# Order of dense matmuls in three FFNs of a two-layer decoder trunk

## The chip, the cores and the metric

The kernel runs on one core of one Trainium2 chip. Its time is what the device takes for one execution, in microseconds. The engines are named as the profile names them: PE is TensorE's matmul, PEld its weight load (the load of the stationary operand), DVE is VectorE, ACT is ScalarE, POOL is GpSimd and SP is SyncE, which here only starts transfers.

## The reference

The program is a trunk of two decoder layers on 256 tokens with 1024 features. A layer is an FFN, a token mixer and a second FFN, each between two RMS norms and added to the residual stream. All four FFNs compute the same, each with weights of its own:

```
def swiglu(h, wg, wu, wd):                      # wg, wu: 1024 x 2816, wd: 2816 x 1024
    return (jax.nn.silu(h @ wg) * (h @ wu)) @ wd

x = x + 0.5 * rms_norm(swiglu(rms_norm(x, pre), wg, wu, wd), post)
```

The two mixers (sliding window and latent attention in layer 0; compressed, selected, sliding and block-sparse attention in layer 1) are not touched.

## The kernel before

Everything is float32, and each dense product is computed from split operands: an operand `a` is held as `a_hi`, its copy in the chip's shorter float32 form, and `a_lo = a - a_hi`. A product of two such operands is three matmuls that add up in one PSUM bank, hi x hi, hi x lo and lo x hi. `three` (line 893) issues them for one chunk of 128 rows of the contraction. In `mm(dst, lhs, rhs, ...)` the second argument is the stationary operand (activations, 128 x 128), the third the moving one (weights, 128 x 512).

The tokens are two row tiles of 128, `t` = 0 and 1. An FFN walks through 11 blocks of 256 hidden features, `jc` = 0 to 10. In a block:

- `gate_up` (TensorE): for each row tile 8 chunks x 3 = 24 matmuls into PSUM bank 4 + t. The 512 columns are 256 of the gate and 256 of the up projection. The last matmul of a tile raises `gu_ready`.
- ScalarE applies silu to the gate half of each tile (line 679), and VectorE multiplies by the up half (line 1356), which raises `h_ready`.
- `down` of the block before (TensorE): 24 matmuls into banks 0 to 3, in two column parts of 512; within a part tile 0 and then tile 1, each 2 chunks x 3 matmuls. After each part `down_used` is raised.
- `turn_h` (TensorE): waits until both tiles of `h` are there and transposes them, 4 matmuls with the identity, into bank 6 (line 982).

TensorE's order is `gate_up(jc)`, `down(jc - 1)`, `turn_h(jc)`, and again. The last block differs: `down(9)` is cut in two by `turn_h(10)`, so that 12 down matmuls stand before the transposes. Blocks 3 to 8 are a loop with two blocks in its body; the others are written out.

Weights are loaded by SyncE, in one queue, two buffers ahead for gate/up and one for down. Each has to be split on the chip: ScalarE writes the hi part (lines 630 and 692), VectorE the lo part (lines 1281 and 1367). This work stands in a fixed order with the rest. For ScalarE it is, in block `jc` (`step` in its `ffn`): the copy of the turned `h` of block jc - 1, the two halves of its down rows, silu of tile 0, **the two halves of the gate/up weights of block jc + 1**, silu of tile 1. VectorE has the same order, with the multiply in place of silu:

```
def step(jc, g, ahead):
    if jc >= 1:
        behind(jc - 1, g)
    mul(jc, 0, g)
    if ahead:
        split_main(n0 + jc + 1, hi=g(2 * (n0 + jc + 1) + 1, 2))
    mul(jc, 1, g)
```

`ahead` is false only in block 10 of the fourth FFN, after which the program has no more gate/up weights. FFNs are numbered `u` = 0 to 3.

Of the kernel before, what the change touches and what calls it, by code (L numbers as in the profile page):

```python
# [37 lines left out]
P = 128  # L38
SEQ = 256
TILES = SEQ // P  # L40
D = 1024
KD = D // P
# [16 lines left out]
FC = FB // P  # L59
# [27 lines left out]
def trunk(nc, a, out):  # L87
# [5 lines left out]
    first_block, n = {}, 0  # L93
# [20 lines left out]
    job_base, n = {}, 0  # L114
# [12 lines left out]
    rstd_base, n = {}, 0  # L127
# [6 lines left out]
    ss_of, n = {}, 0  # L134
# [20 lines left out]
    with ExitStack() as ctx:  # L155
# [6 lines left out]
        ps = ctx.enter_context(nc.psum_tensor("ps", [P, 8, 512], F32))  # L162
# [3 lines left out]
        w_hi = sb("w_hi", [P, 2, MAIN], F32R)  # L166
        w_lo = sb("w_lo", [P, 2, MAIN], F32R)
        raw_down = sb("raw_down", [P, DOWN])
        down_hi = sb("down_hi", [P, DOWN], F32R)
        down_lo = sb("down_lo", [P, DOWN], F32R)  # L170
# [3 lines left out]
        xt_hi = sb("xt_hi", [P, KD, SEQ], F32R)  # L174
        xt_lo = sb("xt_lo", [P, KD, SEQ], F32R)
# [89 lines left out]
        main_hi, main_lo = sem("main_hi"), sem("main_lo")  # L265
        d_hi, d_lo, down_used = sem("d_hi"), sem("d_lo"), sem("down_used")
# [7 lines left out]
        gu_ready, silu_done, h_ready = sem("gu_ready"), sem("silu_done"), sem("h_ready")  # L274
# [26 lines left out]
        def main_view(buf, n, k, width):  # L301

            return buf[:, n % 2, k * 512:k * 512 + width]
# [585 lines left out]
        def _(pe):  # L889
            def mm(dst, lhs, rhs, start, stop):  # L890
                return pe.matmul(dst, lhs, rhs, start=start, stop=stop, skip_group_check=True)  # L891

            def three(dst, lhs_hi, lhs_lo, rhs_hi, rhs_lo, start, stop):
# [2 lines left out]
                mm(dst, lhs_hi, rhs_lo, False, False)  # L896
                return mm(dst, lhs_lo, rhs_hi, False, stop)

            def turn(job, parts):

                if job >= 2:
                    pe.wait_ge(t_done, job - 1)
                for dst, src in parts:
                    ins = pe.transpose(dst, src, ident[0:src.shape[0], 0:src.shape[0]])  # L904
                ins.then_inc(t_ready, 1)
# [25 lines left out]
            def turn_x(s_no, t):  # L931
                def x_is_new(k):
                    if s_no == 0:
                        pe.wait_ge(x_landed[t], 16)
                    else:

                        pe.wait_ge(x_new, 4 * (s_no - 1) + 2 * t + k // (KD // 2) + 1)
                turn_whole(x, t, x_is_new)

            def product(n, t, width, bank, lo=None, chunks=None, midway=None):  # L940

                for k in range(KD):
                    if k == KD // 2 and midway:
                        midway()
                    if chunks is not None:

                        need = max(8 * t + k + 1, (9, 16)[t] if chunks.startswith("out") else 0)
                        pe.wait_ge(xt_done, 16 * TURNS[chunks] + need)  # L950
                    if k % (KD // 2) == 0:

                        half_no = k // (KD // 2)
                        pe.wait_ge(main_lo, (2 * n + 1 if lo is None else lo) + half_no)
                    ins = three(ps[:, bank, 0:width], xt_hi[:, k, t * P:(t + 1) * P], xt_lo[:, k, t * P:(t + 1) * P],
                                main_view(w_hi, n, k, width), main_view(w_lo, n, k, width), k == 0, k == KD - 1)
                return ins

            def ffn(u, s_no, aside=None):
                n0, d0 = first_block[STAGES[s_no]], u * FBLOCKS  # L960
                turn_x(s_no, 0)

                def gate_up(jc, g, between=None):
                    n = n0 + jc
                    first = isinstance(jc, int) and jc == 0
                    for t in range(TILES):
                        if t == 1 and between:
                            between()
                        if d0 + jc >= 1:

                            pe.wait_ge(h_ready, g(2 * (d0 + jc - 1) + t + 1, 2))
                        product(n, t, 512, 4 + t, lo=g(2 * n + 1, 2), chunks=f"norm{s_no}" if first else None,
                                midway=(lambda: turn_x(s_no, 1)) if first and t == 0 else None).then_inc(gu_ready, 1)

                def turn_h(jc, g):
                    pe.wait_ge(h_ready, g(2 * (d0 + jc) + 2, 2))
                    if d0 + jc >= 1:
                        pe.wait_ge(ht_l, g(d0 + jc, 1))
                    for c in range(FC):
                        for t in range(TILES):  # L980
                            at = c * SEQ + t * P
                            ins = pe.transpose(ps[:, 6, at:at + P], h[:, t, c * P:(c + 1) * P], ident[:, :])  # L982
                    ins.then_inc(ht_ready, 1)

                def down(jc, g, parts=(0, 1)):
                    last = jc == FBLOCKS - 1
                    if parts[0] == 0:
                        pe.wait_ge(ht_l, g(d0 + jc + 1, 1))
                    hi, lo = (xt_hi, xt_lo) if last else (ht_hi, ht_lo)


                    order = [(t, part) for t in range(TILES) for part in range(2)]
                    if not last:
                        order = [(t, part) for part in parts for t in range(TILES)]
                    for i, (t, part) in enumerate(order):
                        if t == 0:
                            pe.wait_ge(d_lo, g(2 * (d0 + jc) + part + 1, 2))
                        for c in range(FC):
                            cols = slice(c * D + part * 512, c * D + part * 512 + 512)
                            ins = three(ps[:, 2 * t + part, :], hi[:, c, t * P:(t + 1) * P],  # L1000
                                        lo[:, c, t * P:(t + 1) * P], down_hi[:, cols], down_lo[:, cols],
                                        jc == 0 and c == 0, last and c == FC - 1)
                        if last:
                            ins.then_inc(y_ready, 1)
                        elif i % 2 == 1:
                            ins.then_inc(down_used, 1)

                def fixed(c, k):
                    return c
                gate_up(0, fixed)  # L1010
                if aside:
                    aside()

                gate_up(1, fixed, between=lambda: turn_h(0, fixed))
                down(0, fixed)
                turn_h(1, fixed)
                gate_up(2, fixed)
                down(1, fixed)
                turn_h(2, fixed)
                with pe.Fori(0, (FBLOCKS - PEEL) // 2 - 1) as i:  # L1020
                    for q in range(2):
                        def looped(c, k, i=i):
                            return c + 2 * k * i
                        gate_up(PEEL + q, looped)
                        down(PEEL + q - 1, looped)
                        turn_h(PEEL + q, looped)
                gate_up(FBLOCKS - 2, fixed)
                down(FBLOCKS - 3, fixed)
                turn_h(FBLOCKS - 2, fixed)
                gate_up(FBLOCKS - 1, fixed)  # L1030

                down(FBLOCKS - 2, fixed, parts=(0,))
                turn_h(FBLOCKS - 1, fixed)
                down(FBLOCKS - 2, fixed, parts=(1,))
                down(FBLOCKS - 1, fixed)
# [90 lines left out]
            n = n0 + len(MIX0_BLOCKS)  # L1126
            pe.wait_ge(t_done, job_base["lat"] + 3)
            pe.wait_ge(main_lo, 2 * n + 2)
            for t in range(TILES):
                for b in range(2):  # L1130
                    for k in range(2):
                        cols = slice(k * 768 + b * 384, k * 768 + b * 384 + 384)
                        ins = three(ps[:, 2 + 2 * t + b, 0:384], lat_hi[:, k, t * P:(t + 1) * P],
                                    lat_lo[:, k, t * P:(t + 1) * P], w_hi[:, n % 2, cols], w_lo[:, n % 2, cols],
                                    k == 0, k == 1)
# [8 lines left out]
            for t in range(TILES):  # L1144
                for b in range(2):
                    cols = slice(1536 + b * 512, 1536 + b * 512 + 512)
                    ins = three(ps[:, 2 * t + b, :], lat_hi[:, 2, t * P:(t + 1) * P], lat_lo[:, 2, t * P:(t + 1) * P],
                                w_hi[:, n % 2, cols], w_lo[:, n % 2, cols], True, True)
# [39 lines left out]
            for i in range(2):  # L1188
                n = n0 + 3 + i
# [3 lines left out]
                for m in range(16):  # L1193
# [3 lines left out]
                    cols = slice(m * CMP_HID, (m + 1) * CMP_HID)  # L1197
# [48 lines left out]
            for t in range(TILES):  # L1246
                pe.wait_ge(cmp_t_done, t + 1)
                for g in range(2):
                    ins = mm(ps[:, 6 + t, g * 256:(g + 1) * 256], probt[:, t, g * P:(g + 1) * P],
                             vcmp[:, g, :, :].rearrange("p a d -> p (a d)"), True, True)  # L1250
# [424 lines left out]
```

## Time and profile before

| | |
|---|---|
| time, median of 2 runs | 1098.91 us (1098.15 to 1099.68) |
| span of the profiled execution | 1096.4 us |
| its own time | not given apart; the median is 2.5 us above its span |
| PE busy | 1010.6 us (92%), 4891 matmuls |
| DVE busy | 596.5 us (54%) |
| ACT busy | 498.3 us (45%) |
| mean granted clock of TensorE | 0.976 |

The span runs from the first to the last instruction of one execution. Busy shares are averages over stages that have different limits. Matmuls are pipelined: each is shown with a duration of about 0.39 us although the next one starts after 0.23 us, so the distance between starts, the pitch, is what one costs in a row of them. The granted clock is 1.0 at 2.4 GHz and 0.5 at 1.2 GHz.

### The profile page before, as it was taken

What the parts mean: (1) busy time and instruction counts of PE and PEld (TensorE: products, weight loads), DVE (VectorE), ACT (ScalarE), POOL (GpSimd) and SP (SyncE); (2) the same over time, 40 slices, a digit from 0 to 9 for tenths busy, and PEclk for the clock granted to TensorE, in tenths of its full rate; (3) what the DMA queues carried; (4) which work ended last, traced back from release to release, by engine and by line L of the source; (5) the groups of instructions that cost most, each with busy time, mean ns of one, the idle gap of its engine ahead of it and who ended that gap; (6) DMA issues with size and microseconds to landing.
All of it is one profiled execution on the core that took longest, in us unless ns stands there. A gap on an engine that the chain in (4) does not pass through costs nothing.

```text
span 1096.4 us, 13234 instructions
## 1 busy us (share of the span) xinstructions
PE 1010.6 (92%) x4891; PEld 839.0 (77%) x4891; DVE 596.5 (54%) x891; ACT 498.3 (45%) x767; POOL 54.7 (5%) x112
## 2 busy tenths in 40 slices
PE   6925999969899999999999999999998999999997
PEld 5824888858777888888788888878887878888885
DVE  4414454535686645544665554566757866555454
ACT  6203344327574643433554344355645545434432
POOL 5000000002301000000000000011000000000000
PEclk9976999989999999999999999999998999999999
DMA  9576474663409365646636564544730172656432
GB/s 332 101 144 196 138 230 160 197 150 124 151 1 313 114 217 200 203 145 226 204 123 218 166 230 155 190 157 154 265 120 1 51 238 90 217 173 228 149 121 77
DMA packets 130086, 182.81 MB, mean 167 GB/s; under 512 B 3038, under 2 KB 105528, under 8 KB 130040
## 3 DMA queue, kind: packets, MB, share of 16 engines
q1 hardware_dynamic: 122448, 170.90, 46.7%
q10 hardware_dynamic: 7080, 11.01, 5.2%
q8 instruction: 30, 0.49, 0.2%
q0 software_dynamic: 512, 0.28, 0.1%
q14 instruction: 16, 0.13, 0.0%
HBM read 176.41 MB, written 5.77 MB: 166 GB/s over the span
## 4 chain that ended last, share of the span: by engine, by line
PE 78%; DMA 7%; DVE 7%; ACT 4%; issue 2%; SPq 0%; POOL 0%; ACTq 0%; DVEq 0%; POOLq 0%
PE ps L891 74%; DMA raw<-in_l_ffn_wu 5%; DVE w_lo L1281 2%; DMA raw_down<-in_l_ffn_wd 2%; PE ps L982 2%; ACT w_hi L630 1%; PE ps L1069 1%; DVE down_lo L1367 1%; ACT xt_hi L639 1%; PE ps L928 1%; DVE x L1345 1%; ACT down_hi L692 1%; PE ps L904 1%; SPq L391 0%; DVE xt_lo L1293 0%
## 5 line engine op out<-in xcount | busy, mean ns | idle before, releaser
L891 PE MATMUL ps<-w_hi,xt_hi 128*128 128x512 f32 (+2 forms) x912 | 359.3, 394 | 14.1 <-DVE w_lo L1281 8.4
L891 PE MATMUL ps<-w_hi,xt_lo 128*128 128x512 f32 (+2 forms) x912 | 353.6, 388 | 0.0
L891 PE MATMUL ps<-w_lo,xt_hi 128*128 128x512 f32 (+2 forms) x912 | 353.1, 387 | 0.0
L1281 DVE TENSOR_TENSOR w_lo<-raw,w_hi 128x2048 fp32r<-128x2048 f32 (+3 forms) x120 | 263.2, 2233 | 121.7 <-ACT w_hi L630 121.6
L630 ACT ACTIVATE w_hi<-raw 128x2048 fp32r<-128x2048 f32 (+3 forms) x120 | 217.6, 1864 | 62.8 <-DMA raw<-in_l_ffn_wu 46.9
L891 PEld LDWEIGHTS ps<-w_hi,xt_hi 128*128 128x128 f32 x912 | 172.3, 189 | 49.8 <-issue 11.3
L891 PEld LDWEIGHTS ps<-w_hi,xt_lo 128*128 128x128 f32 x912 | 172.0, 189 | 35.6
L891 PEld LDWEIGHTS ps<-w_lo,xt_hi 128*128 128x128 f32 x912 | 172.4, 189 | 33.0
L891 PE MATMUL ps<-down_hi,ht_hi 128*128 128x512 f32 x320 | 125.7, 393 | 3.6 <-DVE down_lo L1367 3.6
L1367 DVE TENSOR_TENSOR down_lo<-raw_down,down_hi 128x1024 fp32r<-128x1024 f32 x88 | 104.2, 1222 | 44.9 <-ACT down_hi L692 44.9
L891 PE MATMUL ps<-down_lo,ht_hi 128*128 128x512 f32 x320 | 125.2, 391 | 0.0
L891 PE MATMUL ps<-down_hi,ht_lo 128*128 128x512 f32 x320 | 125.2, 391 | 0.0
L1362 DVE TENSOR_TENSOR ht_lo<-ps,ht_hi 128x512 fp32r<-128x512 f32 x40 | 27.7, 692 | 173.6 <-ACT ht_hi L686 173.6
L686 ACT ACTIVATE ht_hi<-ps 128x512 fp32r<-128x512 f32 x40 | 23.9, 599 | 213.0 <-PE ps L982 213.0
L679 ACT ACTIVATE h<-ps,rstd 128x256 f32<-128x256 f32 x88 | 41.7, 474 | 160.6 <-PE ps L891 160.5
L692 ACT ACTIVATE down_hi<-raw_down 128x1024 fp32r<-128x1024 f32 x88 | 88.4, 1052 | 35.4 <-DMA raw_down<-in_l_ffn_wd 23.7
L1356 DVE SCALAR_TENSOR_TENSOR h<-ps,rstd,h 128x256 f32<-128x256 f32 x88 | 42.3, 480 | 85.5 <-ACT h L679 85.5
L891 PEld LDWEIGHTS ps<-down_hi,ht_hi 128*128 128x128 f32 x320 | 60.4, 189 | 16.5 <-issue 4.0
L891 PEld LDWEIGHTS ps<-down_hi,ht_lo 128*128 128x128 f32 x320 | 60.5, 189 | 12.8
L891 PEld LDWEIGHTS ps<-down_lo,ht_hi 128*128 128x128 f32 x320 | 60.5, 189 | 12.5
L982 PE MATMUL ps<-ident,h 128*128 128x128 f32 x176 | 26.8, 275 | 30.3 <-DVE h L1356 30.3
L596 POOL TENSOR_SCALAR meansq<-sumsq 128x1 f32<-128x1 f32 x12 | 4.9, 409 | 901.0 <-ACT ps L663 901.0
(185 smaller groups left out, 789.2 us busy)
## 6 DMA issues: line engine op xcount, KB each, us to landing
raw_down<-in_l_ffn_wd SPq DMA_DIRECT2D x44, 1024.0 KB, 5.0
raw<-in_l_ffn_wg SPq DMA_DIRECT2D x43, 1024.0 KB, 7.3
raw<-in_l_ffn_wu SPq DMA_DIRECT2D x43, 1024.0 KB, 9.8
raw<-in_l_w_in SPq DMA_DIRECT2D x7, 2048.0 KB, 9.7
raw<-in_l_w_out SPq DMA_DIRECT2D x4, 2048.0 KB, 8.1
bias_rows<-logit ACTq DMA_DIRECT2D x3, 1536.0 KB
gpost<-in_l_ffn_post ACTq DMA_DIRECT2D x4, 512.0 KB, 4.2
bias<-bias_rows ACTq DMA_DIRECT2D x1, 2048.0 KB, 10.3
```

What stands on the lines that cost most here:

```text
L630: act.activation(part(w_hi), part(raw), ACT.Copy).then_inc(main_hi, 1)
L639: act.activation(xt_hi[:, k, t * P:(t + 1) * P], xt_bank(t, k), ACT.Copy, **kw).then_inc(xt_h, 1)
L679: act.activation(h[:, t, :], ps[:, 4 + t, 0:FB], ACT.Silu, scale=rstd[:, r:r + 1]).then_inc(silu_done, 1)
L686: act.activation(dst, ps[:, 6, :].rearrange("p (c t) -> p c t", c=FC), ACT.Copy).then_inc(ht_h, 1)
L692: act.activation(down_part(down_hi, part), down_part(raw_down, part), ACT.Copy).then_inc(d_hi, 1)
L891: return pe.matmul(dst, lhs, rhs, start=start, stop=stop, skip_group_check=True)
L904: ins = pe.transpose(dst, src, ident[0:src.shape[0], 0:src.shape[0]])
L982: ins = pe.transpose(ps[:, 6, at:at + P], h[:, t, c * P:(c + 1) * P], ident[:, :])
L1281: dve.tensor_tensor(part(w_lo), part(raw), part(w_hi).bitcast(F32), ALU.subtract).then_inc(main_lo, 1)
L1356: dve.scalar_tensor_tensor(h[:, t, :], ps[:, 4 + t, FB:2 * FB], rstd[:, r:r + 1], h[:, t, :], ALU.mult, ALU.mult).then_inc(h_ready, 1)
L1362: dve.tensor_tensor(lo, ps[:, 6, :].rearrange("p (c t) -> p c t", c=FC), hi.bitcast(F32), ALU.subtract)\
L1367: dve.tensor_tensor(down_part(down_lo, part), down_part(raw_down, part), down_part(down_hi, part).bitcast(F32), ALU.subtract).then_inc(d_l ...
```

## The change

Three edits, one for each of the FFNs `u` = 1, 2 and 3, all of them in TensorE's instructions. The number of matmuls, their operands and the sums that they make are the same.

- `u` = 1: in all gate/up products the three terms of a chunk are issued as hi x hi, lo x hi, hi x lo (stationary x moving), so that the first two have one moving operand.
- `u` = 2: in the down products of blocks 0 to 9 the row tiles alternate matmul by matmul, so that two matmuls in a row have one moving operand and different banks.
- `u` = 3: in the gate/up products of blocks 2 to 10 the row tiles alternate in the same way (`product_of_both`). The wait for `h_ready` now asks for both tiles at once, and `gu_ready` is raised by the last two matmuls, one for each tile.

```diff
--- before.py
+++ after.py
@@ -896,6 +896,15 @@
                 mm(dst, lhs_hi, rhs_lo, False, False)
                 return mm(dst, lhs_lo, rhs_hi, False, stop)
 
+            def terms(lhs_hi, lhs_lo, rhs_hi, rhs_lo):
+                return [(lhs_hi, rhs_hi), (lhs_hi, rhs_lo), (lhs_lo, rhs_hi)]
+
+            def three_moving(dst, lhs_hi, lhs_lo, rhs_hi, rhs_lo, start, stop):
+
+                mm(dst, lhs_hi, rhs_hi, start, False)
+                mm(dst, lhs_lo, rhs_hi, False, False)
+                return mm(dst, lhs_hi, rhs_lo, False, stop)
+
             def turn(job, parts):
 
                 if job >= 2:
@@ -937,7 +946,21 @@
                         pe.wait_ge(x_new, 4 * (s_no - 1) + 2 * t + k // (KD // 2) + 1)
                 turn_whole(x, t, x_is_new)
 
-            def product(n, t, width, bank, lo=None, chunks=None, midway=None):
+            def product_of_both(n, bank, lo):
+
+                last = [None, None]
+                for k in range(KD):
+                    if k % (KD // 2) == 0:
+                        pe.wait_ge(main_lo, lo + k // (KD // 2))
+                    sides = [terms(xt_hi[:, k, t * P:(t + 1) * P], xt_lo[:, k, t * P:(t + 1) * P],
+                                   main_view(w_hi, n, k, 512), main_view(w_lo, n, k, 512)) for t in range(TILES)]
+                    for i in range(3):
+                        for t in range(TILES):
+                            lhs, rhs = sides[t][i]
+                            last[t] = mm(ps[:, bank + t, 0:512], lhs, rhs, k == 0 and i == 0, k == KD - 1 and i == 2)
+                return last
+
+            def product(n, t, width, bank, lo=None, chunks=None, midway=None, three=three):
 
 
 
@@ -963,6 +986,11 @@
                 def gate_up(jc, g, between=None):
                     n = n0 + jc
                     first = isinstance(jc, int) and jc == 0
+                    if u == 3 and isinstance(jc, int) and jc >= 2:
+                        pe.wait_ge(h_ready, g(2 * (d0 + jc - 1) + 2, 2))
+                        for ins in product_of_both(n, 4, g(2 * n + 1, 2)):
+                            ins.then_inc(gu_ready, 1)
+                        return
                     for t in range(TILES):
                         if t == 1 and between:
                             between()
@@ -970,7 +998,8 @@
 
                             pe.wait_ge(h_ready, g(2 * (d0 + jc - 1) + t + 1, 2))
                         product(n, t, 512, 4 + t, lo=g(2 * n + 1, 2), chunks=f"norm{s_no}" if first else None,
-                                midway=(lambda: turn_x(s_no, 1)) if first and t == 0 else None).then_inc(gu_ready, 1)
+                                midway=(lambda: turn_x(s_no, 1)) if first and t == 0 else None,
+                                three=three_moving if u == 1 else three).then_inc(gu_ready, 1)
 
                 def turn_h(jc, g):
                     pe.wait_ge(h_ready, g(2 * (d0 + jc) + 2, 2))
@@ -989,6 +1018,19 @@
                     hi, lo = (xt_hi, xt_lo) if last else (ht_hi, ht_lo)
 
 
+                    if u == 2 and not last:
+                        for part in parts:
+                            pe.wait_ge(d_lo, g(2 * (d0 + jc) + part + 1, 2))
+                            for c in range(FC):
+                                cols = slice(c * D + part * 512, c * D + part * 512 + 512)
+                                sides = [terms(hi[:, c, t * P:(t + 1) * P], lo[:, c, t * P:(t + 1) * P],
+                                               down_hi[:, cols], down_lo[:, cols]) for t in range(TILES)]
+                                for i in range(3):
+                                    for t in range(TILES):
+                                        lhs, rhs = sides[t][i]
+                                        ins = mm(ps[:, 2 * t + part, :], lhs, rhs, jc == 0 and c == 0 and i == 0, False)
+                            ins.then_inc(down_used, 1)
+                        return
                     order = [(t, part) for t in range(TILES) for part in range(2)]
                     if not last:
                         order = [(t, part) for part in parts for t in range(TILES)]
```

TensorE, fourth FFN, start of a gate/up product in the loop. The names are output, moving and stationary operand: `w` the weights, `xt` the turned activations. Before:

```order
L954 REGISTER_ALU [waits h_ready]
L891 MATMUL ps<-w_hi,xt_hi 128x512 [waits main_lo]
L891 MATMUL ps<-w_lo,xt_hi 128x512
L891 MATMUL ps<-w_hi,xt_lo 128x512
L891 MATMUL ps<-w_hi,xt_hi 128x512
L891 MATMUL ps<-w_lo,xt_hi 128x512
L891 MATMUL ps<-w_hi,xt_lo 128x512
```

With the change:

```order
L954 REGISTER_ALU [waits h_ready]
L891 MATMUL ps<-w_hi,xt_hi 128x512 [waits main_lo]
L891 MATMUL ps<-w_hi,xt_hi 128x512
L891 MATMUL ps<-w_lo,xt_hi 128x512 x2
L891 MATMUL ps<-w_hi,xt_lo 128x512 x2
L891 MATMUL ps<-w_hi,xt_hi 128x512 x2
L891 MATMUL ps<-w_lo,xt_hi 128x512 x2
```

Each row of 2 is one term for tile 0 and the same term for tile 1; before, all 24 matmuls of tile 0 came first.

TensorE, the same block, at the end of the down products and at the transposes of `h`. Before:

```order
L891 MATMUL ps<-down_hi,ht_hi 128x512
L891 MATMUL ps<-down_lo,ht_hi 128x512
L891 MATMUL ps<-down_hi,ht_lo 128x512
L976 REGISTER_ALU
L982 MATMUL ps<-ident,h 128x128 [waits ht_l,h_ready]
L982 MATMUL ps<-ident,h 128x128 x3
```

With the change:

```order
L891 MATMUL ps<-down_hi,ht_hi 128x512
L891 MATMUL ps<-down_lo,ht_hi 128x512
L891 MATMUL ps<-down_hi,ht_lo 128x512
L1005 REGISTER_ALU
L1011 MATMUL ps<-ident,h 128x128 [waits ht_l,h_ready]
L1011 MATMUL ps<-ident,h 128x128 x3
```

Nothing moved here except the line numbers: the transposes still stand behind 24 down matmuls and still wait for both tiles of `h`.

TensorE, second FFN, start of a gate/up product in the loop. Before:

```order
L954 REGISTER_ALU [waits h_ready]
L891 MATMUL ps<-w_hi,xt_hi 128x512 [waits main_lo]
L891 MATMUL ps<-w_lo,xt_hi 128x512
L891 MATMUL ps<-w_hi,xt_lo 128x512
L891 MATMUL ps<-w_hi,xt_hi 128x512
L891 MATMUL ps<-w_lo,xt_hi 128x512
L891 MATMUL ps<-w_hi,xt_lo 128x512
```

With the change:

```order
L977 REGISTER_ALU [waits h_ready]
L891 MATMUL ps<-w_hi,xt_hi 128x512 [waits main_lo]
L891 MATMUL ps<-w_hi,xt_lo 128x512
L891 MATMUL ps<-w_lo,xt_hi 128x512
L891 MATMUL ps<-w_hi,xt_hi 128x512
L891 MATMUL ps<-w_hi,xt_lo 128x512
L891 MATMUL ps<-w_lo,xt_hi 128x512
```

The second and third term of each chunk have traded places. The instructions of ScalarE, VectorE, SyncE and GpSimd stay as they were, in number and order.

## Rows read from the trace of the kernel before

**Rows 1.** The page: its first line and the clock that TensorE was granted.
```profile
span 1096.4 us, 13234 instructions
...
PEclk9976999989999999999999999999998999999999
```

**Rows 2.** Busy time by stretch: within the second FFN, within the fourth.
```profile
core 0: us, PE busy (x) PEld busy (x) DVE busy (x) ACT busy (x) POOL busy (x), PEclk, DMA share, GB/s
356.00:537.00 181.00, 180.20 (x818) 148.96 (x819) 96.74 (x95) 82.70 (x93) 2.59 (x4) 1.00 0.56 186
915.00:1083.00 168.00, 167.85 (x761) 138.94 (x762) 83.47 (x72) 68.65 (x71) 0.00 (x0) 1.00 0.49 163
```

**Rows 3.** Timeline of TensorE, fourth FFN, block 5: start us, duration us, then what.
```profile
982.84 0.48 PE L891 MATMUL ps<-w_hi,xt_hi 128*128 128x512 f32 x1
...
988.42 0.39 PE L891 MATMUL ps<-w_hi,xt_hi 128*128 128x512 f32 x1
...
993.40 0.39 PE L891 MATMUL ps<-w_lo,xt_hi 128*128 128x512 f32 x1
993.63 0.39 PE L891 MATMUL ps<-w_hi,xt_lo 128*128 128x512 f32 x1
993.86 0.39 PE L891 MATMUL ps<-down_hi,ht_hi 128*128 128x512 f32 x1
...
999.07 0.39 PE L891 MATMUL ps<-down_hi,ht_lo 128*128 128x512 f32 x1
999.30 0.60 PE L982 MATMUL ps<-ident,h 128*128 128x128 f32 x4
999.65 0.48 PE L891 MATMUL ps<-w_hi,xt_hi 128*128 128x512 f32 x1
```

**Rows 4.** Timeline of TensorE behind two idle stretches and at the half clock.
```profile
58.36 0.47 PE L891 MATMUL ps<-down_hi,ht_hi 128*128 128x512 f32 x1 [3.63 <-DVE down_lo L1367]
...
59.83 0.63 PE L891 MATMUL ps<-down_hi,ht_hi 128*128 128x512 f32 x1
60.26 0.63 PE L891 MATMUL ps<-down_lo,ht_hi 128*128 128x512 f32 x1
...
755.41 0.44 PE L904 MATMUL ps<-ident,xn 128*128 128x128 f32 x2 [1.54 <-DVE logit L1554]
```

**Rows 5.** Timeline of ScalarE, the same block 5.
```profile
988.62 0.47 ACT L679 ACTIVATE h<-ps,rstd 128x256 f32<-128x256 f32 x1 [3.00 <-PE ps L891]
988.99 3.71 ACT L630 ACTIVATE w_hi<-raw 128x2048 fp32r<-128x2048 f32 x2
994.06 0.47 ACT L679 ACTIVATE h<-ps,rstd 128x256 f32<-128x256 f32 x1 [1.36 <-PE ps L891]
```

**Rows 6.** Timeline of VectorE, the same block 5.
```profile
989.12 0.48 DVE L1356 SCALAR_TENSOR_TENSOR h<-ps,rstd,h 128x256 f32<-128x256 f32 x1 [2.06 <-ACT h L679]
990.93 4.49 DVE L1281 TENSOR_TENSOR w_lo<-raw,w_hi 128x2048 fp32r<-128x2048 f32 x2 [1.32 <-ACT w_hi L630]
995.34 0.48 DVE L1356 SCALAR_TENSOR_TENSOR h<-ps,rstd,h 128x256 f32<-128x256 f32 x1
```

**Rows 7.** Timeline, first FFN: a multiply of `h` and the load behind it.
```profile
95.40 0.48 DVE L1356 SCALAR_TENSOR_TENSOR h<-ps,rstd,h 128x256 f32<-128x256 f32 x1
...
95.93 0.71 PEld L982 LDWEIGHTS ps<-ident,h 128*128 128x128 f32 x4 [30.68 <-DVE h L1356]
```

**Rows 8.** Timeline of VectorE, fourth FFN: the first and last of eight split pairs.
```profile
940.51 4.49 DVE L1281 TENSOR_TENSOR w_lo<-raw,w_hi 128x2048 fp32r<-128x2048 f32 x2 [1.32 <-ACT w_hi L630]
...
1058.14 4.50 DVE L1281 TENSOR_TENSOR w_lo<-raw,w_hi 128x2048 fp32r<-128x2048 f32 x2 [1.32 <-ACT w_hi L630]
```

**Rows 9.** The page: transfers of the up weights, us to landing.
```profile
raw<-in_l_ffn_wu SPq DMA_DIRECT2D x43, 1024.0 KB, 9.8
```

**Rows 10.** Busy time at a fall of the clock and around an idle stretch.
```profile
59.80:63.30 3.50, 3.50 (x10) 2.71 (x9) 0.00 (x0) 0.00 (x0) 0.00 (x0) 0.51 0.51 80
752.00:756.00 4.00, 2.46 (x15) 1.89 (x14) 2.77 (x7) 0.60 (x1) 0.00 (x0) 1.00 1.08 360
```

## The prediction

> **What bounds the kernel now.** I read the busy shares first: TensorE works almost without a break and its granted clock is full nearly everywhere [rows 1]. So the question is what a matmul costs and what TensorE waits for. In the windows view the second and the fourth FFN are TensorE from end to end at clock 1.00, with no idle time worth naming [rows 2]. Then I read one block of the fourth FFN on the timeline [rows 3]. A block is 48 gate/up matmuls (the first at 982.84, tile 1 from 988.42), 24 down matmuls (from 993.86) and four transposes of `h` (999.30); the next block starts at 999.65, a period of 16.81 us. Inside one PSUM bank 23 steps take 993.63 - 988.42 = 5.21 us, 0.2265 us each. From 988.42 to 999.07 there are 47 steps, 10.65 us, again 0.2266 us each, though the bank changes four times in them, and though of every three steps one keeps the stationary operand and two change both. Neither the bank nor a repeated stationary operand shows in the pitch. At the half clock a matmul takes 60.26 - 59.83 = 0.43 us [rows 4], which is 512 columns at 1.2 GHz; 512 columns at 2.4 GHz would be 0.2133 us, so 13.3 ns of the warm pitch are something else.
>
> **Part one, second FFN (`three_moving`).** Nothing is added or removed: of 3 matmuls the last two trade places. The last matmul of a product, which releases ScalarE, stays where it was in time. What is new is that the second has the moving operand of the first. No step of the trace before has that, so it has to be bounded. Below: it could lose the 13.3 ns. Above: the dearest mean pitch of a 512-column stretch in rows 3 is the first product of a block, (988.42 - 982.84) / 24 = 0.2325 us, 5.9 ns over the steady one. I take zero, because the steps that do occur cost the same whatever they keep. There are 11 blocks x 16 = 176 such pairs: -2.3 to +1.0 us.
>
> **Part two, third FFN (down products).** 10 blocks x 24 = 240 matmuls now change bank at every step and have 120 pairs with one moving operand. `down_used` is still raised by the twelfth and the twenty-fourth of them, and the waits for `d_lo` stand where they stood, so nobody hears of it earlier or later. By the steps above I take zero, bounds -1.6 (120 x 13.3 ns) to +1.4 us (240 x 5.9 ns).
>
> **Part three, fourth FFN (gate/up products, blocks 2 to 10).** 9 x 48 = 432 matmuls, 216 pairs; by pitch alone zero, bounds -2.9 to +2.5 us. But here a release moves. Before, tile 0 was finished after 24 matmuls and tile 1 after 48; now both are finished by the 47th and 48th. ScalarE and VectorE keep their order: silu and multiply of tile 0, then the two splits of the next block's gate/up weights, then silu and multiply of tile 1. Until now the splits ran beside tile 1's matmuls. Now they start 5.2 us later, and the multiply of tile 1, for which the transposes of `h` wait, stands behind them on VectorE. Worked out on the block of rows 3, 5 and 6:
> - silu starts 0.43 us after the start of a product's last matmul (993.63 to 994.06) [rows 3, 5]. Tile 0's is now the 47th, at 993.40: silu at 993.83.
> - ScalarE's splits start 0.37 us behind (988.62 to 988.99) [rows 5]: 994.20. Silu of tile 1 follows them near 997.8, early enough.
> - VectorE's splits start 1.94 us behind ScalarE's (988.99 to 990.93) [rows 5, 6]: 996.14. The multiply of tile 0 is over by then (994.33 to 994.81).
> - The multiply of tile 1 starts 4.41 us after that (990.93 to 995.34) and takes 0.48 [rows 6]: it ends at 1001.03.
> - TensorE loads `h` 0.05 us after such a multiply ends (95.88 to 95.93) [rows 7], and transposes 0.01 us later: 1001.09 where it was 999.30.
>
> The 24 down matmuls, 5.44 us, cover only part of that chain: **1.79 us of new wait per block**. Queued behind it on TensorE are the transposes and the whole next block, so all of it is on the path. Splits of 4.49 us stand in each of blocks 2 to 9, the first of them as in the block worked out [rows 8], so 8 x 1.79 = **14.3 us**. Block 10 is the last of the program and has no splits after tile 0: its second multiply ends about 1.9 us after its 47th matmul starts, while 12 down matmuls (2.7 us) stand before the transposes. No wait there.
>
> What else hears of the later splits: the transfer of the block after next starts when they are done (SyncE queues the down rows' transfer behind it, needed later still). It takes 9.8 us to land [rows 9] and had a period of 16.8 us; the period grows to 18.6 and its reader moves later by 5.2, so it stays hidden. VectorE and ScalarE do the same work per block in a longer period. The next block's weights are split at about 1000.6, before the transposes end, so `main_lo` is no second wait; should it come later than I think, `main_lo` is late next.
>
> The Trainium skill ("TensorE: Matmul & The Clock Gate", section "Wait — 56ns, not 53.3ns?") has 215.7 ns between starts of 512-column matmuls at the full clock; this trace has 226.6. If the new orders came down to that figure in all 1200 moved matmuls, an estimate by that page would take 13.1 us off the sum and nearly cancel it; that is the fourth rival below. No row here shows a stretch at that pitch.
>
> **The sum.** 0 + 0 + 14.3 us on a span of 1096.4. The two timed runs are 1098.2 and 1099.7, median 1098.9; I put 2.5 us around the span, the difference of the median. 1096.4 + 14.3 + 2.5 = **1113.2 us**, 1.3% slower.
>
> **Rivals.**
> - *The new waits pull the clock down.* TensorE would stand idle from 999.46 (end of the last down matmul) to 1001.09, 1.63 us per block. The trace has an idle of 1.54 us at 755.41 with clock 1.00 around it, and one of 3.63 us at 58.36 after which it fell at about 59.8 [rows 4, 10]. Mine is just beyond the harmless one and far from the other. A fall costs about (1 - 0.51) x 3.5 = 1.7 us [rows 10]. Four falls give 1120.0; one in each of the eight blocks gives 1126.8, which is the case on the other side: slower by over 2%, from the fifth fall on. Chance 0.12, of which 0.05 with five or more.
> - *A repeated moving operand is cheaper.* All 512 pairs save 13.3 ns: -6.8 us, 1106.4. Nothing shows it, nothing excludes it. 0.08.
> - *Alternating banks are dearer* by the 5.9 ns of rows 3, in 672 matmuls: +4.0 us, 1117.2. Against it: four bank changes in rows 3 at the same pitch. 0.07.
> - *The 13.3 ns go in every moved matmul*, because they are the price of a new moving operand into the bank just written and the new orders spare it: 1200 x 13.3 = 16.0 us, 1097.2, not slower. It decides from 14.3 / 1200 = 11.9 ns each. Against it: the steps of rows 3 that do change the bank pay as much as the others. 0.03.
> - *TensorE stumbles over banks and its clock swings.* With a bank change at every step, each group would have a little idle time and the clock would alternate. If half of the 672 matmuls ran at the 0.43 us of rows 4, that is 336 x 0.2 = 67 us, 1180. Against it: the bank changes of rows 3, without a gap. 0.02. The Trainium skill (same page, section "A second HAM failure mode: psum-queue depth-cycling") reports such a kernel.
>
> My forecast has 0.68.
>
> **How the numbers follow.** The prediction is the likeliest case, 1113.2; by itself it would lie within 1110 and 1117. The range 1106 to 1121 takes in the cheaper pairs, the dearer banks and up to four falls of the clock, and leaves out about 0.1 of the chances. A change of 2% (22 us), about what a measurement of this kernel can tell from no change, lies above 1120.9 or below 1076.9: slower 0.08 (five falls or more, the stumble, and a little for the unseen), faster 0.01, within 0.91.
>
> **What would show it.** In the fourth FFN the period is 18.6 us in eight blocks, with an idle of about 1.6 us before each group of transposes, put down to the multiply of `h`, and a tenth block without it. ScalarE's splits start after the gate/up matmuls, not in their middle. In the second and third FFN every pitch is 227 ns, and their lengths stay. I am wrong if a pitch of a pair differs, if the clock row shows falls between 930 and 1085, or if the multiply of tile 1 is there before the down products end.

## The result, and the profile after

The changed kernel takes 1110.18 us, median of 2 runs (1109.94 to 1110.41), against 1098.91 (1098.15 to 1099.68) before: ratio 1.0123, 95% interval [1.0089, 1.0157]. It is slower by 11.3 us. Forecast were 14.3 us and 1113.2.

The first lines of the page after and its clock row, beside [rows 1]:

```profile
span 1108.7 us, 13219 instructions
...
PEclk9967999989999999999999999999989999999999
```

The span grew by 12.3 us. Busy time by stretch follows, within the second, the third and the fourth FFN (columns as in [rows 2]):

```profile
core 0: us, PE busy (x) PEld busy (x) DVE busy (x) ACT busy (x) POOL busy (x), PEclk, DMA share, GB/s
353.68:534.00 180.32, 180.15 (x817) 148.72 (x818) 96.22 (x93) 82.90 (x93) 2.16 (x4) 1.00 0.56 184
543.70:724.00 180.30, 180.25 (x820) 149.22 (x820) 96.68 (x93) 81.40 (x92) 2.23 (x4) 1.00 0.56 190
912.40:1095.00 182.60, 169.54 (x760) 138.13 (x761) 83.01 (x71) 67.54 (x71) 0.00 (x0) 1.00 0.45 150
```

In the second and third FFN TensorE has practically no idle time and its clock is 1.00, as before. From the first transposes of `h` to the last, each of these two FFNs takes 159.87 us; before it was 159.88 and 159.87. In the fourth it was busy throughout [rows 2]; now 182.60 - 169.54 = 13.1 us of the stretch are idle. The wait has a name in the table of waits (total, times, longest), taken over the fourth FFN:

```profile
PE ps L1011 <- DVE h L1398: 13.0, 8, 1.6
```

Eight waits of 1.63 us, for the multiply of `h`. No wait for a transfer stands in that table, and TensorE waits for `w_lo` only once, 0.2 us. Block 5 of that FFN on TensorE's timeline (start, duration, what), beside [rows 3]:

```profile
985.78 0.72 PE L891 MATMUL ps<-w_hi,xt_hi 128*128 128x512 f32 x2
...
996.32 0.62 PE L891 MATMUL ps<-w_hi,xt_lo 128*128 128x512 f32 x2
...
1001.99 0.39 PE L891 MATMUL ps<-down_hi,ht_lo 128*128 128x512 f32 x1
1004.01 0.66 PE L1011 MATMUL ps<-ident,h 128*128 128x128 f32 x4 [1.63 <-DVE h L1398]
1004.42 0.71 PE L891 MATMUL ps<-w_hi,xt_hi 128*128 128x512 f32 x2
```

The last two gate/up matmuls stand in one row from 996.32, so the 47th starts there and the 48th near 996.55. The down products end where they would have; the transposes, due 0.23 us after 1001.99, start at 1004.01. ScalarE in the same block, beside [rows 5]:

```profile
996.75 0.47 ACT L679 ACTIVATE h<-ps,rstd 128x256 f32<-128x256 f32 x1 [8.35 <-PE ps L891]
997.12 3.71 ACT L630 ACTIVATE w_hi<-raw 128x2048 fp32r<-128x2048 f32 x2
1000.73 0.46 ACT L679 ACTIVATE h<-ps,rstd 128x256 f32<-128x256 f32 x1
```

And VectorE, beside [rows 6]:

```profile
997.26 0.48 DVE L1398 SCALAR_TENSOR_TENSOR h<-ps,rstd,h 128x256 f32<-128x256 f32 x1 [7.41 <-ACT h L679]
999.06 4.50 DVE L1323 TENSOR_TENSOR w_lo<-raw,w_hi 128x2048 fp32r<-128x2048 f32 x2 [1.32 <-ACT w_hi L630]
1003.47 0.48 DVE L1398 SCALAR_TENSOR_TENSOR h<-ps,rstd,h 128x256 f32<-128x256 f32 x1
```

Every link of the chain is there: silu 0.43 us after the 47th matmul, splits 0.37 us behind it on ScalarE and 1.94 us later on VectorE, the multiply of tile 1 another 4.41 us later, ending at 1003.95. The next row of TensorE is 0.06 us behind. The splits that used to run under tile 1's matmuls now run under the down products and beyond them.

### The profile page after: what moved, and what is told of

It reads as the page before. It is cut to its first block, busy times and chain, and to the rows that moved or that the text cites. A ratio compares the mean times of both kernels' runs of the same rounds, so it can differ in the third digit from the quotient of the medians.

```text
span 1108.7 us, 13219 instructions
## 1 busy us (share of the span) xinstructions
PE 1012.4 (91%) x4891; PEld 838.8 (76%) x4891; DVE 596.7 (54%) x891; ACT 497.3 (45%) x767; POOL 54.7 (5%) x112
## 4 chain that ended last, share of the span: by engine, by line
PE 75%; DVE 8%; DMA 6%; ACT 5%; issue 4%; POOL 0%; SPq 0%; ACTq 0%; DVEq 0%; POOLq 0%
PE ps L891 71%; DMA raw<-in_l_ffn_wu 4%; DVE w_lo L1323 3%; ACT w_hi L630 2%; PE ps L1011 2%; DMA raw_down<-in_l_ffn_wd 2%; PE ps L1111 1%; DVE down_lo L1409 1%; ACT xt_hi L639 1%; PE ps L937 1%; ACT down_hi L692 1%; PE ps L913 1%; DVE x L1387 0%; DVE h L1398 0%; SPq L391 0%
## 5 line engine op out<-in xcount | busy, mean ns | idle before, releaser
L891 PE MATMUL ps<-w_hi,xt_hi 128*128 128x512 f32 (+2 forms) x912 | 347.5, 394 | 14.0 <-DVE w_lo L1323 8.1
L891 PE MATMUL ps<-w_hi,xt_lo 128*128 128x512 f32 (+2 forms) x912 | 341.4, 387 | 0.0
L891 PE MATMUL ps<-w_lo,xt_hi 128*128 128x512 f32 (+2 forms) x912 | 341.3, 387 | 0.0
L891 PEld LDWEIGHTS ps<-w_hi,xt_hi 128*128 128x128 f32 x912 | 171.5, 189 | 49.6 <-issue 11.3
L891 PE MATMUL ps<-down_hi,ht_hi 128*128 128x512 f32 x320 | 119.6, 394 | 3.7 <-DVE down_lo L1409 3.7
L891 PE MATMUL ps<-down_hi,ht_lo 128*128 128x512 f32 x320 | 119.1, 392 | 0.0
L891 PE MATMUL ps<-down_lo,ht_hi 128*128 128x512 f32 x320 | 119.0, 392 | 0.0
L891 PEld LDWEIGHTS ps<-down_lo,ht_hi 128*128 128x128 f32 x320 | 60.7, 190 | 12.6
L1011 PEld LDWEIGHTS ps<-ident,h 128*128 128x128 f32 x176 | 21.4, 141 | 49.9 <-DVE h L1398 45.4
```

## The experiments

Ratios are to the kernel before, run beside each kernel on the same chip, with their 95% intervals. That kernel had medians of 1096.3 to 1096.7 us in these comparisons. A ratio under 1 means less time. The first three kernels take the change apart.

### Only the second FFN's edit

```
-  if u == 2 and not last:                 +  if u == 9 and not last:
-  if u == 3 and ... jc >= 2:              +  if u == 9 and ... jc >= 2:
```

No FFN has the number 9, so these two conditions switch the other edits off.

> Only the edit in the second FFN (lo x hi as the second term). Theory A, the matmul order costs nothing by itself and only a late release does: no change, ratio 1.000 within 0.002, pitch 227 ns for all steps, the second FFN as long as before. Rival B, a repeated moving operand is cheaper: up to 2.3 us less (176 pairs x 13.3 ns), ratio 0.998, and pitches of 213 ns between the first two terms. Rival C, the 2.8 us by which the changed kernel was ahead of the kernel before when its second FFN began belong to the code and not to chance: the same lead here.

Measured: 1.0002 [0.9988, 1.0016]. No change. The order of terms costs and gives nothing. Its profiled execution came to the second FFN 2.4 us earlier than that of the kernel before (353.98 against 356.41 us for the first gate/up matmul), but the ratio of its ten runs shows no such lead: what looked like one is chance of single executions.

### Only the third FFN's edit

```
-  three=three_moving if u == 1 else three  +  three=three
-  if u == 3 and ... jc >= 2:               +  if u == 9 and ... jc >= 2:
```

> Only the edit in the third FFN (down products alternate row tiles). Theory A: no change, ratio 1.000 within 0.002, every pitch 227 ns although each matmul changes the bank. Rival B, alternating costs or saves: -1.6 to +1.4 us. Rival C, the lead before the second FFN belongs to the code: 2.8 us less, ratio 0.9975.

Measured: 0.9999 [0.9989, 1.0010]. No change. Its profiled execution reached the same point at 355.79 us.

### Only the fourth FFN's edit

```
-  three=three_moving if u == 1 else three  +  three=three
-  if u == 2 and not last:                  +  if u == 9 and not last:
```

> Only the edit in the fourth FFN (gate/up products alternate row tiles). Theory A: all of the loss is here. Eight waits of 1.79 us and about 0.1 us more each for the transposes behind them, 15.1 us: 1114.0 where the start of the program goes as in the kernel before, 1111 where it has the lead of the changed kernel; ratio 1.010 to 1.014, and the same ratio to the kernel before as the full change within 0.003. Rival: part of the loss comes from the other two edits, then this ratio is clearly under 1.010.

Measured: 1.0137 [1.0115, 1.0158], 1111.0 us. All of the loss is here, 15.0 us of 1096.3. The interval goes from 12.6 to 17.3 us. The full change's 1.0123 [1.0089, 1.0157] agrees with it. In the trace there are again eight waits, 13.0 us.

### The multiply ahead of the splits

```
 def step(jc, g, ahead):                    # ScalarE; VectorE alike with mul
     ...
     silu(jc, 0, g)
+    if u == 3 and jc >= 2:
+        silu(jc, 1, g)
     if ahead:
         split_main(n0 + jc + 1, g)
-    silu(jc, 1, g)
+    if not (u == 3 and jc >= 2):
+        silu(jc, 1, g)
```

> The full change, and in the fourth FFN from block 2 on ScalarE and VectorE handle tile 1 (silu, multiply) before the two splits of the next weights. Same instructions. Theory A: h is ready about 1.5 us after the gate/up products, under the 5.4 us of down products, the eight waits are gone, ratio 1.000 within 0.002, fourth FFN back to 16.8 us per block. Rival, the alternation itself costs something beside the wait: the fourth FFN stays longer by up to 2.5 us, and with pitches over 227 ns. Second rival, the splits now come late and the next block waits for the lo part of its weights: up to 1.4 us per block, 11 us in all.

Measured: 1.0003 [0.9990, 1.0015]. TensorE's instructions are those of the changed kernel, and the loss is gone. VectorE in a block of the fourth FFN, the two multiplies in one row and the splits behind them:

```profile
989.58 0.88 DVE L1401 SCALAR_TENSOR_TENSOR h<-ps,rstd,h 128x256 f32<-128x256 f32 x2 [7.28 <-ACT h L679]
991.75 4.49 DVE L1326 TENSOR_TENSOR w_lo<-raw,w_hi 128x2048 fp32r<-128x2048 f32 x2 [1.29 <-ACT w_hi L630]
```

TensorE at the end of that block:

```profile
994.31 0.39 PE L894 MATMUL ps<-down_hi,ht_lo 128*128 128x512 f32 x1
994.54 0.60 PE L1014 MATMUL ps<-ident,h 128*128 128x128 f32 x4
994.90 0.71 PE L894 MATMUL ps<-w_hi,xt_hi 128*128 128x512 f32 x2
```

`h` is ready at 990.46, four microseconds before the transposes want it, and these start without a wait, 0.23 us after the start of the last down matmul. Both rivals fall: the alternation costs nothing beside its release, and the splits, now the last of the block, are in time for the next one.

### Half of the splits ahead

```
+    if ahead and u == 3 and jc >= 2:
+        split_main(n0 + jc + 1, g, which=(0,))
+        silu(jc, 1, g)
+        split_main(n0 + jc + 1, g, which=(1,))
+        return
```

> The full change, but in the fourth FFN from block 2 on ScalarE and VectorE do only the first of the two splits before silu and multiply of tile 1, and the second behind. Theory A: the multiply of tile 1 ends about 2.2 us earlier than in the changed kernel, 0.4 us before the down products are over, so no wait is left: ratio 1.000 within 0.002. Rival, the wait is not from the splits: 1.010 to 1.014 as with the full change.

Measured: 0.9988 [0.9976, 1.0001]. VectorE: first split, multiply of tile 1, second split:

```profile
991.63 2.29 DVE L1330 TENSOR_TENSOR w_lo<-raw,w_hi 128x2048 fp32r<-128x2048 f32 x1 [1.32 <-ACT w_hi L632]
993.84 0.48 DVE L1405 SCALAR_TENSOR_TENSOR h<-ps,rstd,h 128x256 f32<-128x256 f32 x1
994.24 2.28 DVE L1330 TENSOR_TENSOR w_lo<-raw,w_hi 128x2048 fp32r<-128x2048 f32 x1
```

TensorE's transposes in that block:

```profile
994.79 0.60 PE L1018 MATMUL ps<-ident,h 128*128 128x128 f32 x4
```

The multiply ends at 994.32, the transposes are due at 994.79: 0.47 us to spare where 0.4 was worked out. With one split less before it, 2.29 us of work, the multiply comes 2.2 us earlier in relation to the transposes: 0.47 us early instead of 1.73 us late. So the wait follows the length of the work that stands before the multiply and is cut off at zero.

### Tile 0 done earlier

```
-                    for i in range(3):
-                        for t in range(TILES):
-                            ...
+                    pairs = [(i, t) for i in range(3) for t in range(TILES)]
+                    if k >= 6:
+                        pairs = [(i, 0) for i in range(3)]
+                    for i, t in pairs:
+                            ...
+                for k in (6, 7):           # and now tile 1 of these chunks
+                    ...
```

> The full change, but in the alternating gate/up products only chunks 0 to 5 alternate; then come the 6 matmuls of tile 0 for chunks 6 and 7, then those of tile 1. Tile 0 is released 5 matmuls earlier than in the changed kernel, 1.13 us. Theory A: the wait shrinks from 1.79 to 0.65 us per block, so 8 x (0.65 + 0.1) = 6 us over the kernel before: ratio 1.0055, 1102 to 1105 us depending on the start of the program. Rival, the wait hangs on alternating as such: 1.010 or more; rival, all or nothing: 1.000.

Measured: 1.0060 [1.0043, 1.0077], 6.5 us, 1102.98 us. TensorE at the end of a block:

```profile
997.13 0.39 PE L891 MATMUL ps<-down_hi,ht_lo 128*128 128x512 f32 x1
998.01 0.66 PE L1017 MATMUL ps<-ident,h 128*128 128x128 f32 x4 [0.49 <-DVE h L1404]
```

The wait is 998.01 - 997.13 - 0.23 = 0.65 us, to the digit. A release 1.13 us earlier on TensorE's side made it 1.14 us shorter.

### Alternating in all four FFNs

The edits of the multiply ahead of the splits and of both alternations, with these conditions:

```
-  if u == 3 and isinstance(jc, int) and jc >= 2:
+  if isinstance(jc, int) and jc >= 2 and (u == 3 or jc < FBLOCKS - 1):
-  if u == 2 and not last:
+  if not last:
```

> All four FFNs alternate row tiles in the down products of blocks 0 to 9 and in the gate/up products of blocks 2 to 9 (in the fourth also 10), 2544 matmuls in all, with silu and multiply of tile 1 ahead of the splits in those blocks; no product has the order of the second FFN's edit. Theory A, order is free: ratio 1.000 within 0.002, pitch 227 ns. Rival, a bank change or a repeated moving operand has a price: 1 ns each would be 2.5 us, 5.9 ns each 15 us, a saving of 13.3 ns per pair 17 us less.

Measured: 0.9975 [0.9963, 0.9988], faster by 2.8 us, which neither the theory nor the rival had. The pitch first: three stretches without a wait, in the second, third and fourth FFN, columns as above:

```profile
400.00:500.00 100.00, 100.00 (x454) 82.75 (x453) 48.65 (x43) 41.08 (x42) 0.00 (x0) 1.00 0.57 189
600.00:700.00 100.00, 100.00 (x454) 82.77 (x453) 49.47 (x42) 40.80 (x43) 0.00 (x0) 1.00 0.55 187
930.00:1070.00 140.00, 140.00 (x634) 115.88 (x633) 66.67 (x57) 55.50 (x56) 0.00 (x0) 1.00 0.52 173
```

TensorE was busy to the last digit, 454 matmuls in 100 us, clock 1.00; the steps between starts are 226 and 227 ns. The second, the third and the fourth FFN each take 159.87 or 159.88 us from their first transposes to their last, as in the kernel before. So alternating costs nothing here, and the gain lies elsewhere: in the first FFN, where TensorE stood still for 30 us behind a late transfer of weights. VectorE there, both multiplies and then the splits that waited for that transfer:

```profile
59.91 0.87 DVE L1401 SCALAR_TENSOR_TENSOR h<-ps,rstd,h 128x256 f32<-128x256 f32 x2
90.04 4.50 DVE L1326 TENSOR_TENSOR w_lo<-raw,w_hi 128x2048 fp32r<-128x2048 f32 x2 [29.26 <-ACT w_hi L630]
```

TensorE, the transposes and the first matmul of the next block:

```profile
67.19 0.60 PE L1014 MATMUL ps<-ident,h 128*128 128x128 f32 x4
92.39 1.22 PE L894 MATMUL ps<-w_hi,xt_hi 128*128 128x512 f32 x2 [24.60 <-DVE w_lo L1326]
```

And in the kernel before, VectorE's splits and the same first matmul, for which its multiply and the transposes had to come first:

```profile
90.99 4.49 DVE L1281 TENSOR_TENSOR w_lo<-raw,w_hi 128x2048 fp32r<-128x2048 f32 x2 [31.24 <-ACT w_hi L630]
...
96.70 0.78 PE L891 MATMUL ps<-w_hi,xt_hi 128*128 128x512 f32 x1
```

From the start of VectorE's splits to that matmul it is 96.70 - 90.99 = 5.71 us before and 92.39 - 90.04 = 2.35 us here, 3.4 us less. With the multiply done ahead, the transposes fall into the wait, and TensorE starts as soon as the first half of the weights is split.

### The same order of work without any alternation

```
     silu(jc, 0, g)                         # in the kernel before; VectorE alike
+    if 2 <= jc < FBLOCKS - 1:
+        silu(jc, 1, g)
     if ahead:
         split_main(n0 + jc + 1, g)
-    silu(jc, 1, g)
+    if not (2 <= jc < FBLOCKS - 1):
+        silu(jc, 1, g)
```

> The kernel before, matmuls in their old order everywhere, and in blocks 2 to 9 of all four FFNs silu and multiply of tile 1 ahead of the two splits. Theory: the 2.8 us that the alternating kernel with this order gained come from the first FFN, where block 2's multiply no longer stands behind splits that wait some 30 us for a transfer; TensorE transposes during that wait and starts the next block with the first half of its weights: about 3.4 us less there, nothing elsewhere, ratio 0.997. Rival: the gain came from the alternation of the matmuls, then 1.000 here. Second rival: with the old order the later splits cost something in the steady blocks, then over 1.000.

Measured: 0.9982 [0.9971, 0.9994], 1.8 us. The gain is there without an alternating matmul, so it comes from the order on ScalarE and VectorE. It is smaller than the 3.4 us worked out, which lie outside the interval (0.7 to 3.2 us).

### And in the first FFN alone

As the last one, with `u == 0 and 2 <= jc < FBLOCKS - 1`.

> The kernel before, with silu and multiply of tile 1 ahead of the splits in blocks 2 to 9 of the first FFN alone. Theory: the same gain as with all four FFNs, ratio 0.997, since in the others the multiply is in time either way. Rival: the gain is spread over the FFNs, a quarter of it here, 0.9993.

Measured: 0.9977 [0.9965, 0.9990], 2.5 us. The rival's 0.9993 lies outside the interval: as far as the intervals tell, one FFN gives all of the gain. The trace shows the early start without any alternation. VectorE's splits and TensorE's first matmul behind them:

```profile
91.03 4.49 DVE L1284 TENSOR_TENSOR w_lo<-raw,w_hi 128x2048 fp32r<-128x2048 f32 x2 [30.06 <-ACT w_hi L630]
...
93.37 0.80 PE L894 MATMUL ps<-w_hi,xt_hi 128*128 128x512 f32 x1 [26.43 <-DVE w_lo L1284]
```

That is 2.34 us, as in the kernel that alternates everywhere. Not all of the 3.4 us arrives further on. From the start of these splits to the transposes of the next block it is 24.06 us in the kernel before and 23.07 to 23.72 us in the seven others whose first FFN is as before, against 21.04 us here, 21.06 us in the kernel of the last section and 20.16 us in the one that alternates everywhere. These 2.0 to 3.9 us agree with the measured 1.8 to 2.8. The 1.0 us between the kernel before and the changed one is that of the clock: TensorE starts again at the half clock, and the full clock came back at 100.7 us in the kernel before, 4.0 us after the first matmul, and at 98.5 us in the changed kernel, 2.0 us after it.

This kernel and the one that alternates everywhere are the fastest of the study, by a quarter of a per cent against the kernel before; between the two the intervals tell no difference.

### Gate/up alternation in all four FFNs, work in its old order

```
-  if u == 3 and isinstance(jc, int) and jc >= 2:
+  if isinstance(jc, int) and jc >= 2:
```

> The full change with the gate/up alternation in all four FFNs, ScalarE and VectorE as in the kernel before. Theory A: each of the three further FFNs gets eight waits (15.1 us) and, in its block 10, which there has splits and only 12 down matmuls behind it, one of about 4.5 us: 3 x 19.6 + 15.1 = 74 us, about 1173 us, ratio 1.067. The wait of block 10 is longer than the 3.63 us idle after which the clock fell before; if the clock falls there, 1.7 us more each, 1178 us. Rival, the cost has to do with the first blocks or the length of the program and not with the release: clearly under 1160.

Measured: 1.0648 [1.0631, 1.0666], 1168.0 us, 71 us slower where 74 were worked out. The working had eight waits of 1.79 us in every FFN; the trace has seven in the first, since that of block 2 coincides with the wait of 29 us behind the late transfer. That takes 1.9 us off, which leaves 72. Two waits of this kernel on TensorE's timeline, in block 10 of the second FFN and in a middle block of the third:

```profile
568.89 0.66 PE L1011 MATMUL ps<-ident,h 128*128 128x128 f32 x4 [4.35 <-DVE h L1398]
...
667.34 0.66 PE L1011 MATMUL ps<-ident,h 128*128 128x128 f32 x4 [1.63 <-DVE h L1398]
```

The stretches right behind the three waits of 4.35 us (in block 10 of the first three FFNs) and behind that last one, columns as above:

```profile
248.70:252.20 3.50, 3.50 (x11) 2.93 (x12) 0.00 (x0) 0.00 (x0) 0.00 (x0) 0.51 0.67 194
569.70:573.20 3.50, 3.50 (x10) 2.72 (x9) 0.96 (x2) 0.48 (x1) 0.00 (x0) 0.52 0.00 0
781.30:784.80 3.50, 3.50 (x11) 2.92 (x12) 1.66 (x2) 0.60 (x1) 0.00 (x0) 0.52 0.84 269
668.60:672.10 3.50, 3.50 (x10) 2.72 (x9) 3.06 (x3) 1.92 (x3) 0.00 (x0) 0.51 0.00 0
```

In this execution the clock fell for some 3.4 us after each of the three waits of 4.35 us. Of the 31 waits of 1.63 us that lie in this kernel's blocks 2 to 9, one was followed by a fall, this one; in the changed kernel and in the one with the fourth FFN's edit alone none of 16 was. The fall cost that block 1.65 us (18.81 us became 20.46).

The traced execution is the slowest of four: 1172.37 us at a mean granted clock of 0.969, the others 1167.54 to 1168.12 us at 0.975. An estimate from these figures, twice the missing clock times the span, gives 73 us at the half clock in the traced one and 58 us in the others, 14 us less. They have no trace, but they cannot all have had these falls: the three in three are those of one execution.

The idle time of 3.63 us in [rows 4] teaches the same. All twelve kernels have it, between 3.52 and 3.70 us long. In ten traces the clock fell during it or soon behind it; in two it did not, here in the one with only the second FFN's edit:

```profile
58.91 0.47 PE L891 MATMUL ps<-down_hi,ht_hi 128*128 128x512 f32 x1 [3.59 <-DVE down_lo L1409]
...
60.00:64.00 4.00, 4.00 (x20) 3.30 (x19) 0.29 (x1) 0.00 (x0) 0.00 (x0) 1.00 0.51 81
```

## Why the prediction was right

**Parts one and two, zero.** Right. In the second FFN the second term now repeats the moving operand of the first (`w_hi,xt_hi`, then `w_hi,xt_lo`), and nothing comes of it: the FFN takes 159.87 us from its first transposes to its last:

```profile
400.95 0.40 PE L891 MATMUL ps<-w_hi,xt_hi 128*128 128x512 f32 x1
401.19 0.39 PE L891 MATMUL ps<-w_hi,xt_lo 128*128 128x512 f32 x1
401.41 0.39 PE L891 MATMUL ps<-w_lo,xt_hi 128*128 128x512 f32 x1
401.64 0.40 PE L891 MATMUL ps<-w_hi,xt_hi 128*128 128x512 f32 x1
```

In the third FFN two matmuls with one moving operand and different banks stand in one row; a pair takes 0.45 us, two pitches, and this FFN too takes 159.87 us as before:

```profile
587.01 0.62 PE L891 MATMUL ps<-down_lo,ht_hi 128*128 128x512 f32 x2
587.47 0.61 PE L891 MATMUL ps<-down_hi,ht_lo 128*128 128x512 f32 x2
587.92 0.62 PE L891 MATMUL ps<-down_hi,ht_hi 128*128 128x512 f32 x2
588.37 0.62 PE L891 MATMUL ps<-down_lo,ht_hi 128*128 128x512 f32 x2
```

Apart, the edits measured 1.0002 and 0.9999. The rivals of a cheaper pair, of a dearer bank change, of the vanished 13.3 ns and of a TensorE that stumbles over banks are gone, the last two by the 2544 matmuls that alternate in FFNs of unchanged length. The figure of 215.7 ns in the Trainium skill ("TensorE: Matmul & The Clock Gate", section "Wait — 56ns, not 53.3ns?") was reached by none of these orders.

**Part three, 1.79 us in eight blocks.** Right in place, count and size: 1004.01 - 1001.99 - 0.23 = 1.79. Block 10 has no wait. The measured cost of the fourth FFN is larger by 0.7 us: from its first transposes to its last it took 159.87 us before and takes 174.88 after, 15.0 us. The rest is the first step behind each wait. The next block's first matmul came 999.65 - 999.30 = 0.35 us after the transposes [rows 3]; now it comes 0.41 us after them in the block shown and 0.56 us in another:

```profile
1022.65 0.66 PE L1011 MATMUL ps<-ident,h 128*128 128x128 f32 x4 [1.63 <-DVE h L1398]
1023.21 0.49 PE L891 MATMUL ps<-w_hi,xt_hi 128*128 128x512 f32 x1
```

I had moved the transposes as a whole and not asked what the first steps behind a wait take.

**The sum.** 1113.2 was 3.0 us too high, although those 0.7 us are missing from it. Two things outweigh them. I put the median's 2.5 us around the span; a run's time is about 1.7 us above its own span (1110.41 and 1108.7), and the profiled execution of the kernel before was the one of 1098.15. This error of 0.8 us and the missing 0.7 us cancel by luck. And up to the second FFN, in code that no edit touches, the profiled execution after was 2.7 us ahead (353.68 against 356.41 at its first gate/up matmul). Of these, 0.2 us were there when TensorE started again behind the 30 us wait, 1.0 us came in the block behind it, where the clock came back sooner, and the rest, some 1.5 us, between the last transposes of the first FFN and the first of the second; what made that part is open. The executions of the three parts lie between (353.98, 355.79, 354.06), and two of these kernels measure as unchanged: this is the spread of single executions. The two runs of the kernel before were also 2.2 to 2.6 us above its medians in the experiments. There, with more runs, the fourth FFN's edit alone costs 15.0 us, for which 14.3 was a better forecast than the 11.3 of the result suggests; the full change was not measured again.

**The clock.** The rival at 0.12 did not occur in the changed kernel, but it was not far off: the same wait was followed by a fall once in the 47 of three traces.

**What hears of it.** The weights' transfers stayed hidden, as did `main_lo`: TensorE waited 0.2 us for it in the whole fourth FFN. What I missed is upstream: the order silu, splits, multiply has a price in the kernel before too, in the block of the first FFN where the splits wait 31 us for a transfer.

## What to carry to other kernels

A reordering of matmuls has to be read by what it releases and when: interleaving two accumulations cost TensorE nothing here, but it delivers the first result at the time of the second, and everything that other engines had queued between the two moves with it. Write down, for each engine, what stands between the late release and the instruction that TensorE waits for, and compare it with the matmuls that cover it; if it doesn't fit, move the short work that is waited for ahead of the long work that is not. The same exchange can pay where the long work is itself held up by a transfer; here it gave 2.5 us in a kernel without any alternation.

## What the runs showed of the hardware

- The pitch of these 128 x 512 matmuls at the full clock is 226.6 ns, 13.3 ns more than 512 columns at 2.4 GHz, and in the orders tried here it doesn't depend on a repeated moving or stationary operand or on the bank. What the 13.3 ns are stays open.
- The first gate/up matmul starts 0.35 us after the transposes where these follow matmuls, and 0.41 or 0.56 us after them where they follow a wait of 1.63 us: 0.06 or 0.2 us more.
- An idle time of 4.35 us was followed by a fall of the clock three times in three in the one traced execution, but by their mean clock the other three cannot all have had these falls; one of 3.5 to 3.7 us ten times in twelve; one of 1.63 us once in 47. So the length of one gap does not decide alone; what else does was not tried.
